# Adding up one-hot slices with the identity matrix on TensorE instead of halving them on VectorE

## The reference, cut to what matters

```
s1, i1 = lax.top_k(s[:, :, 0], PEER_TOPK)
s2, i2 = lax.top_k(s[:, :, 1], PEER_TOPK)
cand = (s1[..., :, None] + s2[..., None, :]).reshape(T, N_PEER_HEADS, PEER_TOPK * PEER_TOPK)
cand_idx = (i1[..., :, None] * N_KEYS + i2[..., None, :]).reshape(...)
top_s, pos = lax.top_k(cand, PEER_TOPK)
idx = jnp.take_along_axis(cand_idx, pos, axis=-1)
g = jax.nn.softmax(top_s.astype(jnp.float32), axis=-1)
a = jax.nn.gelu(jnp.einsum('tkd,td->tk', expert_u[ix], hx), approximate=False)
return jnp.einsum('tk,tkd->td', gx * a, expert_v[ix])
```

## Time and profile before

| | |
|---|---|
| median of 3 runs | 1820.45 us |
| the profiled execution's own time | 1815.94 us |
| its span, first to last instruction | 1813.9 us |
| mean granted TensorE clock | 0.966 |
| busy: PE, DVE, POOL, ACT | 92%, 83%, 51%, 36% of the span |
| building the dense tables | from 567.2 to 707 us |
| its first, second and third block | 45.4, 44.4, 50.0 us |

### The profile page before, as it was taken

One profiled execution on the slowest core, in us unless ns is written; L12 is line 12 of the kernel. 1 busy time (PEld: TensorE's weight loads), 2 busy tenths in 40 slices (PEclk: granted clock), 3 DMA queues, 4 the chain that ended last, 5 costly groups with the idle time before them and its releaser, 6 DMA issues.

```text
span 1813.9 us, 28223 instructions
## 1 busy us (share of the span) xinstructions
PE 1665.3 (92%) x9322; PEld 1442.0 (79%) x9338; DVE 1506.1 (83%) x3069; ACT 645.6 (36%) x1085; POOL 916.1 (51%) x771
## 2 busy tenths in 40 slices
PE   4999998999954886899999999999999999999994
PEld 2776766479953886799999999999999999999993
DVE  0732266457999999799999999999999999999997
ACT  1212266121103785233333333333333333333331
POOL 1101000013402665777778877777666666666661
PEclk9999999999976998999999999999999999999997
DMA  9445202140010668999999999999999999999993
GB/s 355 173 163 208 75 1 98 42 184 3 1 47 1 187 186 253 385 406 409 407 408 390 402 409 409 409 409 409 409 408 409 409 409 403 410 409 407 406 397 124
DMA packets 198137, 518.28 MB, mean 286 GB/s; under 512 B 14643, under 2 KB 64435, under 8 KB 197941
## 3 DMA queue, kind: packets, MB, share of 16 engines
q0 software_dynamic: 73728, 268.47, 37.3%
q1 hardware_dynamic: 122320, 245.59, 36.3%
q10 hardware_dynamic: 2022, 3.38, 0.5%
HBM read 486.45 MB, written 30.93 MB: 285 GB/s over the span
## 4 chain that ended last, share of the span: by engine, by line
PE 79%; DVE 10%; DMA 5%; issue 3%; ACT 3%; POOL 0%; SPq 0%; POOLq 0%; ACTq 0%; DVEq 0%; PEldq 0%; another core or an unknown queue 0%
PE ps L1786 20%; PE ps L1785 20%; PE ps L1784 19%; PE ps L1758 4%; PE ps L1873 4%; DMA arena_w<-in_w_mod 2%; PE ps L1599 2%; PE ps L1603 2%; PE ps L1600 2%; PE ps L1697 2%; DMA arena_w<-in_w_in 1%; ACT arena_w L867 1%; DVE arena L1470 1%; PE ps L1721 1%; DVE arena L1307 1%
## 5 line engine op out<-in xcount | busy, mean ns | idle before, releaser
L1786 PE MATMUL ps<-hT_hi,U_lo 128*128 128x384 f32 x1024 | 344.3, 336 | 0.0
L1784 PE MATMUL ps<-hT_hi,U_hi 128*128 128x384 f32 x1024 | 344.1, 336 | 0.0
L1785 PE MATMUL ps<-hT_lo,U_hi 128*128 128x384 f32 x1024 | 343.5, 335 | 0.0
L537 POOL DMA_INDIRECT rows_under<-in_expert_u,idxn x192 | 273.8, 1426 | 116.4 <-issue 41.8
L1784 PE MATMUL ps<-hT_hi,C_hi 128*128 128x512 f32 x768 | 301.2, 392 | 14.5 <-DVE C_lo L1447 14.5
L537 POOL DMA_INDIRECT rows_under<-in_expert_v,idxn x192 | 242.7, 1264 | 140.4 <-DVE arena L1470 77.8
L1786 PE MATMUL ps<-hT_hi,C_lo 128*128 128x512 f32 x768 | 303.2, 395 | 0.0
L1785 PE MATMUL ps<-hT_lo,C_hi 128*128 128x512 f32 x768 | 303.1, 395 | 0.0
L1470 DVE SCALAR_TENSOR_TENSOR arena<-rows_under,dots,arena 128x1024 f32<-128x1024 f32 x192 | 247.8, 1291 | 4.8
L930 ACT ACTIVATE act_t<-ps 128x384 f32<-128x384 f32 x128 | 63.0, 492 | 386.2 <-PE ps L1786 386.2
L1784 PEld LDWEIGHTS ps<-hT_hi,U_hi 128*128 128x128 f32 x1024 | 192.6, 188 | 4.9
(11 more groups left out here) (273 smaller groups left out, 3010.9 us busy)
## 6 DMA issues: line engine op xcount, KB each, us to landing
U_in<-in_expert_uT SPq DMA_DIRECT2D x128, 512.0 KB, 8.7
arena<-in_expert_v SPq DMA_DIRECT2D x128, 512.0 KB, 6.5
arena_w<-in_w_mod SPq DMA_DIRECT2D x12, 2048.0 KB, 12.4
gate_in<-gates_scratch SPq DMA_DIRECT2D x62, 384.0 KB, 7.9
gates_scratch<-arena_w SPq DMA_DIRECT2D x5, 4096.0 KB, 16.6
arena_w<-in_w_in SPq DMA_DIRECT2D x4, 2048.0 KB, 8.7
arena_w<-in_w_query SPq DMA_DIRECT2D x4, 2048.0 KB, 10.8
arena_w<-in_w_out SPq DMA_DIRECT2D x2, 2048.0 KB, 8.4
```

The source lines that it names most:

```text
L537: pool.indirect_dma_start(out=rowr[row], out_offset=None, in_=table, in_offset=bass.IndirectOffsetOnAxis(ap=idxn[:, g, row:row + 1], axis= ...
L1784: nc.tensor.matmul(out, hi, rhi, start=start, stop=False)
L1785: nc.tensor.matmul(out, hi, rlo, start=False, stop=False)
L1786: return nc.tensor.matmul(out, lo, rhi, start=False, stop=stop)
```

## The change

The sums by halving go for n = 0 to 3; only the last choice (n=4) keeps them. PE adds the 16 slices instead, in `pick`: 16 bf16 products with the identity that accumulate in PSUM. For w=0 and n<3 the slice is the stationary operand, so the sum comes out transposed, where `selT_fill` put it by a transpose of its own (one of its two is gone). The key's square parts are made by ACT (`key_squares`), except the last subtraction, which stays on DVE in a new function `finish` behind the softmax weights. For n=3 `finish` copies both sums out of PSUM. A second buffer takes the slices of w=1; `stack_fill` and `stack_out` move two quads later.

```diff
+            def key_squares(n):
+                act.wait_ge(s_picked, 2 * n + 2)
+                if n:
+                    act.wait_ge(s_stackfill, n)
+                    act.wait_ge(s_key2, n)
+                act.copy(key2[:, 0, :], ps[:, 0, 256:384]).then_inc(s_keysq0, 1)
+                act.activation(square, ps[:, 0, 256:384], ACT.Square).then_inc(s_keysq0, 1)
+                act.wait_ge(s_keysq0, 2 * n + 2)
+                act.copy(key2[:, 1, :], square).then_inc(s_keysq, 1)
...
             share_exps(0)
+            key_squares(0)
             stack_out(1)
...
-                if b < NDEN and p == 25:
+                if b < NDEN and p == 23:
+                    key_squares(b)
+                if b < NDEN and p == 27:
                     stack_out(b + 1)
...
-                if n:
-                    dve.wait_ge(s_selfill, min(n, NDEN))
                 for w in range(2):
                     gate_quads(bd, share[2 * w])
...
-                    eqs = note(dve.tensor_tensor(o4, o4, idxf[:, w].unsqueeze(2).broadcast_to([P, TOPK, TOPK, PH]), ALU.mult))
-                    gate_quads(bd, share[2 * w + 1])
-                    dve.wait_ge(s_step, eqs)
+                    eqs = dve.tensor_tensor(o4, o4, idxf[:, w].unsqueeze(2).broadcast_to([P, TOPK, TOPK, PH]), ALU.mult)
+                    if n < LATE_PICK:
+                        eqs.then_inc(s_eqs, 1)
+                        gate_quads(bd, share[2 * w + 1])
+                        continue
+                    link(eqs)
...
+            def finish(n):
+
                 if n < NDEN:
-                    dve.tensor_copy(key2[:, 0, :], sel[:, 1, :])
-                    link(dve.tensor_tensor(square, sel[:, 1, :], sel[:, 1, :], ALU.mult))
-                    link(dve.tensor_copy(key2[:, 1, :], square))
+                    dve.wait_ge(s_keysq, n + 1)
                     dve.tensor_tensor(key2[:, 2, :], square, key2[:, 1, :], ALU.subtract).then_inc(s_key2, 1)
...
+                elif n < LATE_PICK:
+                    dve.wait_ge(s_picked, 2 * n + 2)
+                    dve.tensor_copy(sel[:, 1, :].rearrange("p (h j) -> p h j", h=PH), spread(ps[:, 0, 256:384]).rearrange("p j h -> p h j"))
+                    dve.wait_ge(s_step, note(dve.tensor_copy(sel[:, 0, :].rearrange("p (h j) -> p h j", h=PH),
+                                                             spread(ps[:, 0, 384:512]).rearrange("p j h -> p h j"))))
+                    choice_rows(n, sel[:, 0, :], sel[:, 1, :])
...
                 gate_weights(n)
+                finish(n)
                 gate_quads(bd, weights_share[1])
...
+            def pick(n, w):
+
+                pe.wait_ge(s_eqs, 2 * n + w + 1)
+                if n and w == 0:
+                    pe.wait_ge(s_selT, n)
+                if n and w == 1:
+                    pe.wait_ge(s_keysq, n)
+                for j in range(TOPK):
+                    if w == 0 and n < NDEN:
+                        last = nc.tensor.matmul(ps[:, 0, 0:P], onehots[0][:, j, :], identb, start=(j == 0), stop=(j == TOPK - 1))
+                    else:
+                        at = 256 if w else 384
+                        last = nc.tensor.matmul(ps[:, 0, at:at + P], identb, onehots[w][:, j, :],
+                                                start=(j == 0), stop=(j == TOPK - 1))
+                last.then_inc(s_picked, 1)
...
-                if q % QUADS == 24 and q // QUADS + 1 < NDEN:
+                if q % QUADS in (16, 21):
+                    pick(q // QUADS + 1, (q % QUADS - 16) // 5)
+                if q % QUADS == 26 and q // QUADS + 1 < NDEN:
                     stack_fill(q // QUADS + 2)
```

More of the change, by code:

```diff
@@ L38 @@
 SPARSE = (4, 0)
+LATE_PICK = 4
 RPB = 4
@@ L228, in program @@
                 cutout(BO + 3072, 512).rearrange("p (t n) -> p t n", t=QUAD)]
-        onehot = cutout(BO + 4096, 1024).bitcast(bf16).rearrange("p (j s) -> p j s", j=TOPK)
+        onehots = [cutout(lo, 1024).bitcast(bf16).rearrange("p (j s) -> p j s", j=TOPK) for lo in (BO + 4096, MO + 3072)]
         besti = cutout(XO, 1280).bitcast(u32).rearrange("p (b h w j) -> p b h w j", b=NBLK, h=PH, w=2)
@@ L244, in program @@
         identb = cutout(XO + 4864, 64).bitcast(bf16)
-        square = cutout(BO + 4096, P)
+        square = cutout(XO + 4928, P)
         stack = cutout(BO + 3584, 512).bitcast(bf16).rearrange("p (b g n) -> p b g n", b=2, g=4)
@@ L1358, in select, with choice_rows @@
                                            spread(onehot[:, 1]), ALU.add))
+                if ORDER[n] in SPARSE and n >= LATE_PICK:
+                    choice_rows(n, sel[:, 0, :], sel[:, 1, :])
+            def choice_rows(n, first, second):
+                dve.scalar_tensor_tensor(out=idx[:, SPARSE.index(ORDER[n]), :], in0=first, scalar=float(NKEY), in1=second,
+                                         op0=ALU.mult, op1=ALU.add).then_inc(s_idx, 1)
+            def finish(n):
                 if n < NDEN:
-                    dve.tensor_copy(key2[:, 0, :], sel[:, 1, :])
-                    link(dve.tensor_tensor(square, sel[:, 1, :], sel[:, 1, :], ALU.mult))
-                    link(dve.tensor_copy(key2[:, 1, :], square))
+                    dve.wait_ge(s_keysq, n + 1)
                     dve.tensor_tensor(key2[:, 2, :], square, key2[:, 1, :], ALU.subtract).then_inc(s_key2, 1)
-                if b in SPARSE:
-                    dve.scalar_tensor_tensor(out=idx[:, SPARSE.index(b), :], in0=sel[:, 0, :], scalar=float(NKEY), in1=sel[:, 1, :],
-                                             op0=ALU.mult, op1=ALU.add).then_inc(s_idx, 1)
+                elif n < LATE_PICK:
[3 more added lines that the diff above has]
+                                                             spread(ps[:, 0, 384:512]).rearrange("p j h -> p h j"))))
+                    choice_rows(n, sel[:, 0, :], sel[:, 1, :])
             def gate_weights(n):
@@ L1373, in gate_weights @@
                 link(dve.reciprocal(gsum[:, 0, :], gsum[:, 0, :]))
-                dve.tensor_tensor(gates[:, min(b, 1), :].rearrange("p (h j) -> p h j", h=PH), top[:, n],
+                dve.tensor_tensor((spread(gates[:, 1, :]).rearrange("p j h -> p h j") if n < NDEN else
+                                   gates[:, min(b, 1), :].rearrange("p (h j) -> p h j", h=PH)), top[:, n],
                                   gsum[:, 0, :].unsqueeze(2).broadcast_to([P, PH, TOPK]), ALU.mult).then_inc(s_gate, 1)
@@ L1402, in choose @@
                 gate_weights(n)
+                finish(n)
                 gate_quads(bd, weights_share[1])
             def split_u(n, r):
+                if isinstance(n, int) and n == 1:
+                    dve.wait_ge(s_picked, 2 * LATE_PICK)
                 dve.wait_ge(s_uhi, n + 1)
@@ L1848, in selT_fill @@
                     pe.wait_ge(s_selT, b - 1)
-                for w, src in enumerate((sel[:, 0, :], gates[:, 1, :])):
-                    last = nc.tensor.transpose(ps[:, 0, w * P:(w + 1) * P], src, ident[:, :])
-                last.then_inc(s_selfill, 1)
+                nc.tensor.transpose(ps[:, 0, P:2 * P], gates[:, 1, :], ident[:, :]).then_inc(s_selfill, 1)
             def differences(q):
@@ L1879, in _ @@
             pe.wait_ge(s_curve, 5)
+            pick(0, 0)
+            pick(0, 1)
             stack_fill(1)
```

7 lines of the change are left out of this document (6 added, 1 removed).

## The result

The changed kernel takes 1824.63 us (median of 13 runs, 1822.03 to 1827.54) against 1818.73 us of the kernel before on the same chip (13 runs): a ratio of 1.0031 (95% interval 1.0022 to 1.0040), or 5.6 us more (4.0 to 7.3). The number is close to that of the rival in which PE stays at the upper clock (5.4 us).

The account below looks back on a forecast made before the run. PE's chain of quads, not busy DVE, was taken to bound a block's end. Blocks 1 and 2 lose 11.4 us together, block 3 1.5, the first choice gains 2.0: 10.9 us later, 1831.3 us, range 1823.5 to 1838.

Parts of the forecast that it names:

- the rival in which PE stays at the upper clock: PE's clock does not fall through the pauses: 5.4 us late, 1825.9 us; chance 0.13.
- What bounds the kernel: At a block's end PE's order of quads has no slack and DVE has, despite DVE's 41.4 of 44.4 us busy.
- DVE's own account: Rival: DVE's won work and its wait at the subtraction decide; 2.1 us a block, 1824 us; chance 0.08.
- The rival with exposed weight loads: Weight loads of PE's picks are not hidden: each pick 1.5 us more, 19.9 us late, 1840.4 us; chance 0.09.
- The rival on the other side: DVE is the bound and the wait in `finish` never blocks: 14.6 us gained, 1805.9 us; chance 0.08.
- The new wait: Blocks 1 and 2: DVE's subtraction waits for ACT with quad 24 queued behind it; PE pauses 3.25 us.
- The slow quads: Blocks 1 and 2, behind the pause: PE's lower clock makes two quads slow, 1.8 us a block.
- `stack_out` and the tail: Blocks 1 and 2: `stack_out` ahead of quad 28's eviction puts some 0.1 us on ACT's way to the copy.
- What PE gets: Blocks 1 and 2: two picks of 1.0 us each on PE make quad 23 start 0.6 us late.
- the removed work: DVE loses 4.75 us a block in blocks 1 and 2; only 0.57 us at quad 21 is on the path.
- Block 3: Third block: the second pick, DVE's copies and splits hold up quad 24; 1.5 us late.
- The first choice: First choice, with nothing to hide behind: stack filling begins at 564.45 instead of 566.45, a gain of 2.0 us.

Follow-up runs that it names:

- before_no_sums: The kernel before with the halving sums left out in choices 1 and 2 and nothing in their place: 1815.32 us, 0.9988 of the kernel before.
- late_sub: The changed kernel with DVE's subtraction behind quads 24 to 26 of DVE's order instead of ahead of 24: 1815.28 us, 0.9979 of the kernel before.
- early_picks: The changed kernel with picks behind quads 11 and 17, ACT's parts four quads earlier, stack filling and `stack_out` two earlier: 1812.93 us, 0.9976 of the kernel before.
- after: The changed kernel itself, first set of runs and first profile: 1824.63 us, 1.0031 of the kernel before.
- warm_fill: The changed kernel with 44 extra identity products on PE behind quad 23 of blocks 1 and 2: 1821.43 us, 1.0021 of the kernel before.
- after_again: The changed kernel, unchanged, in a later set of runs for a second profile: 1827.41 us, 1.0054 of the kernel before.
- double_pick: The changed kernel with every pick of n = 1 to 3 issued twice: 1831.21 us, 1.0091 of the kernel before.

## Why the prediction was right in kind and wrong in size

- **What bounds the kernel: held.** The end of a block hangs on PE's order of quads. before_no_sums takes 3.2 us off DVE in a block, and the blocks change by -1.4 and +0.4 us. The rival "DVE's own account" gave 2.1 us a block, measured are 4.1 and 4.2. The rival with exposed weight loads (19.9 us) fell with the pick of 0.89 us, and the one in which PE stays at the upper clock with the slow quads behind the pause. The rival on the other side (1805.9) fell with DVE's wait of 6.30 us; late_sub and early_picks show that even without the pause the gain is 4 us, not 14.6.
- **The new wait: held.** The pause was put at 3.25 us, it is 3.30 and 3.29. From quad 23 to quad 24 it takes 4.6 us instead of 1.1, 3.5 more. The slow quads, put at 1.8, cost 1.65 in all four such pauses of the two profiles. `stack_out` and the tail, from quad 28 to the next block: 0.24 instead of 0.1.
- **What PE gets: the step that failed.** The pick was sized well (1.0 forecast, 0.89 measured), but "quad 23 starts at 648.85 instead of 648.28: 0.6 us late" did not come: quad 23 was 1.25 and 1.1 us early in the first profile's blocks 1 and 2. Two things were missing from this term, and both were put at nothing. The first is the start of the block. All six blocks of the kernel before, in two profiles, have slow quads behind the wait ahead of quad 5; blocks 1 and 2 of the first profile after have none, and quad 7 starts 1.4 to 1.7 us earlier. The waits tell only half of why: block 1 waited 0.9 us there, block 2 as long as before, 2.71 us. I had carried these slow quads over without a word.

The second is POOL. From quad 7 to quad 19 the kernel before goes at POOL's pace: each fourth quad is POOL's, and PE takes it up 0.1 us after POOL is done. Like is compared with like where quads 5 and 6 are slow too, as in warm_fill's second block: its quad 23 stands at 35.45 us, 0.2 us early in spite of two picks. POOL's quads 11 and 15 in warm_fill, and quad 11 in the kernel before:

```profile
631.80 3.56 POOL L558 TENSOR_SCALAR arena<-iota,arena 128x128 f32<-128x128 f32 x4 [5.43 <-PE ps L1921]
...
636.69 3.96 POOL L558 TENSOR_SCALAR arena<-iota,arena 128x128 f32<-128x128 f32 x4 [1.33 <-PE ps L1921]
```
```profile
628.33 3.72 POOL L557 TENSOR_SCALAR arena<-iota,arena 128x128 f32<-128x128 f32 x4 [5.43 <-PE ps L1873]
```

Quad 11 takes 3.56 instead of 3.72, quad 15 3.96 instead of 4.45, together 0.65 us, and PE's quad 15 comes that much earlier (24.63 for 25.31). The prediction counted nothing here because with the picks PE would come to quads 11 to 19 no sooner than POOL; but the picks stand behind quads 16 and 21 and delay neither quad 11 nor quad 15. That is the "nothing" of my sum: 0.6 late, less 0.65, less 0.2 for the two cheaper picks, gives 0.25 early, and 0.2 was measured. The Trainium skill (SBUF — State Buffer, section Who interferes with whom) says that a DVE instruction with two SBUF inputs contends with a POOL one that reads SBUF. Quad 11 agrees, since the sum of w=0 ran beside it before. Quad 15 had no sum beside it in either kernel, only the look-up w=1, whose first operation is this, in the kernel before and in warm_fill:

```profile
635.96 1.21 DVE L1350 TENSOR_TENSOR arena<-arena,places 128x2048 bf16<-128x2048 bf16 x1
```
```profile
638.76 1.22 DVE L1367 TENSOR_TENSOR arena<-arena,places 128x2048 bf16<-128x2048 bf16 x1
```

POOL ended its quad 1.87 us after this start before, and 1.89 after it in warm_fill. In 23 of the 24 blocks of the eight profiles with the picks or sums at their places it was 1.87 to 1.89 us; the exception is the second block of before_no_sums (3.22). So the end of quad 15 goes with DVE's look-up, and what differs is how far into the quad the look-up falls: 2.58 us before, 2.07 in warm_fill. DVE comes to it earlier because the sum of w=0 no longer stands ahead of it: in the first block of before_no_sums, where nothing but the sums is gone, it falls 2.13 us into the quad, and PE's quad 15 starts at 24.45 us instead of 25.29. So this half microsecond of DVE's removed work was on PE's path, by way of POOL. The prediction had 0.57 us of the removed work on the path; that block won 1.4.
- **Per block, then:** -1.2 (quad 23) + 3.5 (the pause) + 1.65 (the slow quads) + 0.24 (the tail) = 4.2 where 5.7 was forecast. Were quads 5 and 6 slow as before, it would be 5.2, as in after_again's block 1. Two blocks make 3.2 us of the 2.9 by which the stretch was over-estimated; the rest cancels.
- **Block 3: +2.0 and, in the second profile, +1.8, for 1.5.** DVE's splits hold up quad 24 as described; three quads behind the pause are slow, where I counted two. In late_sub and warm_fill, after the same 3.22 us, none is, and the block takes 49.0 and 49.1 us, less than before. So the +2.0 hangs on the slow quads. After:

```profile
696.37 1.05 PE L1921 MATMUL ps<-arena,arena_w 128*128 128x128 f32 x8
...
700.86 2.05 PE L1921 MATMUL ps<-arena_w 128*128 128x128 f32 x8 [3.22 <-issue]
...
703.12 1.91 PE L1921 MATMUL ps<-arena_w 128*128 128x128 f32 x8
...
705.26 1.65 PE L1921 MATMUL ps<-rhs_more,arena_w 128*128 128x128 f32 x8
```

- **The first choice: held.** 2.3 us won for 2.0 (2.8 in the second profile). Here nothing hides the sums, and the removed work is gained. The picks and the stack filling:

```profile
556.87 1.86 PE L1888 MATMUL ps<-arena 128*128 128x128 bf16 x16 [23.68 <-DVE arena L1369]
...
559.17 1.89 PE L1891 MATMUL ps<-arena 128*128 128x128 bf16 x16 [0.44 <-DVE arena L1369]
...
562.25 0.62 PE L1875 MATMUL ps<-arena 128*32 128x128 bf16 x12 [1.19 <-DVE arena L1391]
```

PE is at its lower clock (0.50 in the first window), and a pick takes 1.9 us (1.7 forecast).
- **From the stretch to the whole.** The forecast of +10.9 met +8.0 in the stretch and between +5.6 and +9.8 in the times. What separates these two lies mostly ahead of the stretch: the same kernel's two profiles differ by 6.7 us, 0.4 of it in the stretch and 5.7 before it. Why is open.

**What stays open:** why the wait ahead of quad 5 brings the lower clock in some executions and not in others. Waits of 2.70 and 2.71 us did not (after, block 2; after_again, block 2; before_no_sums, block 2), waits of 2.69, 2.42 and, in warm_fill, 2.70 did:

```profile
626.71 1.82 PE L1921 MATMUL ps<-arena_w 128*128 128x128 f32 x8 [2.70 <-issue]
```

The granted clock from the block's start up to this wait was 1.00 both in warm_fill's second block and in that of after (the window up to 622.84 shown above), so it had not fallen before. It is worth 1.1 us a block (49.54 against 48.44), most of the distance between the 4.2 us measured and the 5.7 forecast. Of blocks 1 and 2, three of four had no slow quads there in the two profiles of after, and none of four without them before; but in late_sub, warm_fill and double_pick, whose order at the start of a block is that of after, all six had them. So it is not simply a property of the change, and so few profiles don't tell what it hangs on. Over all profiles, slow quads followed in 22 of the 26 blocks with an unfilled wait of 1.86 to 2.76 us ahead of quad 5; the four without had waits of 2.70 to 2.76. In block 1 of the first profile after, the wait was only 0.91 us.

## What to carry to other kernels

Work taken off an engine with a high busy share is worth only what the chain that ends last had waited for it, also by way of a third engine. Here 4.75 of DVE's 41.4 us went, and with the two picks that replaced them on PE a block became 0.1 to 0.3 us shorter; the one instruction left behind in the wrong place cost 5.2. When a step is handed to another engine, look at what is queued behind the instruction that collects its result, and put that instruction where its wait is already over, or behind the work that others need. Add to each stall what follows it at the lower clock, and check first whether the stalls already in the program will stay as they are.

## What the runs showed of the hardware

- Sixteen accumulating products of 128 by 128 in bf16, each with its own weight load, took 1.06 us as one row and 0.89 us from start to start; at the lower clock 1.86 to 1.89 us.
- After PE's idle 3.3 us in blocks 1 and 2 two of the next three quads ran slowly (granted clock 0.57 in the window shown), in 6 of 6 cases (the two profiles of after, and double_pick). The same time with 2.62 us of products in it left the clock at 1.00, in both blocks. After idle times of 2.7 us both outcomes were seen, and after 3.22 us too: in the third blocks of late_sub (below) and warm_fill no slow quad followed, and they took 49.0 and 49.1 us. So one row of a pause doesn't say what the clock will do.

```profile
697.67 1.13 PE L1926 MATMUL ps<-arena_w 128*128 128x128 f32 x8 [3.22 <-issue]
```
- A POOL quad of four instructions took 3.1 us where DVE stood idle for most of it, 3.96 to 4.45 beside part of the look-up, and 5.51 with both of its large operations beside it.
